# A seven-product scheme for the down projection of a convolutional FFN, in fp32 on one NeuronCore

## What is computed

```python
D_FF = 2816
def conv_ffn(a, w_up, conv_w, w_down):
    g, u = jnp.split(dwconv3(a @ w_up, conv_w), 2, axis=-1)
    return (jax.nn.silu(g) * u) @ w_down

# in both layers of second_block:
h = h + g2 * conv_ffn(modulate(rms_norm(h, norm_ffn[i]), sh2, sc2), ffn_w_up[i], ffn_conv[i], ffn_w_down[i])
```

## Time and profile before

| | kernel before |
|---|---|
| median of 3 runs | 2008.44 us |
| the profiled execution: time / span | 2007.74 / 2006.0 us |
| PE busy | 1888.5 us (94%), 19216 matmul records |
| PEld busy | 1634.6 us (81%), 19216 load records |
| DVE busy | 823.5 us (41%), 1430 instructions |
| ACT busy | 371.6 us (19%) |
| mean granted TensorE clock | 0.976 of 2.4 GHz |
| HBM read | 463.29 MB, 231 GB/s over the span |

### The profile page before, as it was taken

One profiled execution on the slowest core, in us unless ns is written; L12 is line 12 of the kernel. 1 busy time (PEld: TensorE's weight loads), 2 busy tenths in 40 slices (PEclk: granted clock), 3 DMA queues, 4 the chain that ended last, 5 costly groups with the idle time before them and its releaser, 6 DMA issues.

```text
span 2006.0 us, 41961 instructions
## 1 busy us (share of the span) xinstructions
PE 1888.5 (94%) x19216; PEld 1634.6 (81%) x19216; DVE 823.5 (41%) x1430; ACT 371.6 (19%) x691; POOL 25.1 (1%) x24
## 2 busy tenths in 40 slices
PE   6999987989998999997999999999999999999999
PEld 3788776889997788686899996667888778878878
DVE  3868786100004767764000004665675111233210
ACT  3012232100003021322000013361111110021100
POOL 0000200000000000200000000000000000000000
PEclk8999988999999999998999999999999999999999
DMA  9994546699994581562999991204787444434320
GB/s 356 387 385 147 203 166 266 251 375 405 420 411 172 206 316 63 210 237 103 376 387 422 422 392 54 84 2 163 260 295 278 139 145 139 155 126 160 124 74 21
DMA packets 180598, 466.09 MB, mean 232 GB/s; under 512 B 5152, under 2 KB 55680, under 8 KB 172288
## 3 DMA queue, kind: packets, MB, share of 16 engines
q1 hardware_dynamic: 180192, 463.83, 62.1%
q10 hardware_dynamic: 288, 0.52, 0.1%
HBM read 463.29 MB, written 1.05 MB: 231 GB/s over the span
## 4 chain that ended last, share of the span: by engine, by line
PE 86%; DVE 9%; ACT 2%; issue 2%; DMA 1%; SPq 1%; DVEq 0%; ACTq 0%
PE pair L366 84%; DVE AR L1517 2%; DMA ring<-in_ada_w 1%; PE pair L1005 1%; DVE RST L1572 1%; DVE AR L1755 1%; ACT AR L1239 1%; DVE XH L1517 1%; SPq L257 0%; DVE AR L1765 0%; PE pair L874 0%; DVE AR L1769 0%; DVE XH L1756 0%; DVE AR L1809 0%; DVE XH L1579 0%
## 5 line engine op out<-in xcount | busy, mean ns | idle before, releaser
L366 PE MATMUL pair<-AR,ring 128*64 128x88 f32 (+1 forms) x13632 | 772.0, 254 | 30.1 <-issue 16.2
L366 PEld LDWEIGHTS pair<-AR,ring 128*64 128x64 f32 (+1 forms) x13632 | 727.7, 143 | 72.9 <-issue 23.2
L366 PE MATMUL pair<-XH,ring 128*128 128x256 f32 (+1 forms) x3328 | 752.2, 387 | 19.1 <-ACT XH L1140 17.3
L366 PEld LDWEIGHTS pair<-XH,ring 128*128 128x128 f32 (+1 forms) x3328 | 629.9, 191 | 126.2 <-issue 30.1
L2004 DVE TENSOR_TENSOR AR<-AR,pair 128x352 f32<-128x352 f32 x32 | 16.7, 521 | 427.8 <-PE pair L366 427.8
L1517 DVE SCALAR_TENSOR_TENSOR AR<-ring,CACT,AR 128x512 f32<-128x512 f32 x245 | 184.2, 752 | 8.7
L366 PE MATMUL pair<-AR 128*64 128x128 f32 (+5 forms) x768 | 103.0, 330 | 6.5 <-ACT AR L1406 3.3
L366 PEld LDWEIGHTS pair<-AR 128*64 128x64 f32 (+3 forms) x768 | 76.8, 165 | 18.5 <-issue 4.2
L2105 DVE SCALAR_TENSOR_TENSOR AR<-pair,VEC,AR 128x255 f32<-128x255 f32 x88 | 41.9, 476 | 114.4 <-ACT AR L1431 114.4
L1339 ACT ACTIVATE AR<-pair 128x704 f32 (+1 forms) x32 | 24.4, 762 | 308.7 <-PE pair L366 308.7
L1431 ACT ACTIVATE AR<-pair,VEC 128x256 f32<-128x256 f32 x88 | 36.5, 465 | 224.0 <-PE pair L366 224.0
(11 more groups left out here) (256 smaller groups left out, 1091.1 us busy)
## 6 DMA issues: line engine op xcount, KB each, us to landing
ring<-in_ada_w SPq DMA_DIRECT2D x48, 2048.0 KB, 13.0
ring<-in_w_gate SPq DMA_DIRECT2D x32, 2048.0 KB, 10.7
ring<-in_w_up SPq DMA_DIRECT2D x32, 2048.0 KB, 10.8
ring<-in_w_down SPq DMA_DIRECT2D x32, 2048.0 KB, 11.3
ring<-in_ffn_w_up SPq DMA_DIRECT2D x44, 1024.0 KB, 7.6
ring<-in_w_in SPq DMA_DIRECT2D x18, 2048.0 KB, 14.2
ring<-in_ffn_w_down SPq DMA_DIRECT2D x8, 2048.0 KB, 7.8
ring<-in_sc_w_in SPq DMA_DIRECT2D x6, 2048.0 KB, 7.9
```

The costliest lines, as they stand in the source:

```text
L366: return pe.matmul(o, lhsT, rhs, start=start, stop=stop, **kw)
```

## The change

`A` and each chunk of weights are seen as 2 x 2 blocks. For the activations, the index k is the parity of the input tile and h the half of the tokens (128 each); for a weight chunk, k is the same parity and m one half (256 columns) of the 512 output features. For each output half and each of the three chunks (now 4, 4 and 3 pairs of input tiles) seven products of quarter size are formed, in place of the eight of the plain scheme: with sums of weight blocks (S1 = a21 + a22, S2 = S1 - a11, S3 = a11 - a21, S4 = a12 - S2) and sums of activation blocks (T1 = b12 - b11, T2 = b22 - T1, T3 = b22 - b12, T4 = b21 - T2). VectorE makes the weight sums for every chunk (`weight_sums`, 4 operations of up to 128 x 1024) and the activation sums once for each of three groups of an FFN (`token_sums`, 4 operations of up to 128 x 512). Each matmul has a 64-column weight tile and 128 moving columns. The seven products accumulate over the chunks in separate regions of PSUM; `output` adds each of them into `X`, 20 VectorE operations for each half. Half 0 now writes banks 4 to 7, half 1 banks 1 to 5.

The waits are new as well: half 0 starts when the convolution has read tiles up to 19 instead of 21; products 6 and 3 wait for sums of weights; product 4 of half 1's first chunk waits for half 0's output; the DVE starts half 1's output after product 5 of the last chunk. VectorE's program has `token_sums` ahead of the convolution of tiles 10 and 18, and the first chunk's weight sums ahead of tile 20. Besides, some semaphores without use are dropped and two of the start are joined.

The diff, cut to this:

```diff
+TH = S // 2
+DOWN_PAIRS = ((0, 4), (4, 4), (8, 3))
+
+
+BANK_OF = [{1: (4, 4), 6: (4, 4), 7: (5, 5), 5: (5, 5), 2: (6, 6), 3: (6, 6), 4: (7, 7)},
+           {1: (1, 1), 6: (1, 1), 7: (2, 2), 5: (2, 2), 2: (3, 3), 3: (3, 3), 4: (4, 5)}]
+SECOND_IN_BANK = (6, 5, 3)
...
+        SX = [AR[:, 1024 * b:1024 * b + 1024].rearrange("p (t n) -> p t n", t=4) for b in (6, 7, 8)]
+        T1 = XH[:, 2048:2048 + 11 * TH].rearrange("p (t n) -> p t n", t=11)
+        T2 = AR[:, 9 * 1024:9 * 1024 + 11 * TH].rearrange("p (t n) -> p t n", t=11)
+        T4 = AR[:, 9 * 1024 + 11 * TH:9 * 1024 + 22 * TH].rearrange("p (t n) -> p t n", t=11)
+
+        def token_blocks(a, n):
+
+            v = a[:, 0:2 * n * S].rearrange("p (t k h n) -> p t k h n", k=2, h=2, n=TH)
+            return [v[:, :, k, h, :] for k in range(2) for h in range(2)]
+
+        def weight_blocks(c, n):
+
+            v = ring[c % RING][:, 0:2 * n * 512].rearrange("p (t k m n) -> p t k m n", k=2, m=2, n=S)
+            return [v[:, :, k, m, :] for m in range(2) for k in range(2)]
+
+        def of_product(hf, n, m):
+
+            b = BANK_OF[hf][n][m]
+            a = 512 * (b % 2) + S * (n in SECOND_IN_BANK) + TH * m
+            return pair[b // 2][:, a:a + TH]
+
...
-                A = AR[:, 0:22 * N].rearrange("p (t n) -> p t n", n=N)
+                b11, b12, b21, b22 = token_blocks(AR, 11)
                 for hf in range(2):
 
-                    if hf == 0:
-                        pe.wait_ge(s["cv_conv"], 2 * (done_tiles + 22))
-                    for k, (a, nk) in enumerate(((0, 8), (8, 8), (16, 6))):
+                    pe.wait_ge(s["cv_conv"], 2 * (done_tiles + (20, 22)[hf]))
+                    for k, (p0, n_p) in enumerate(DOWN_PAIRS):
                         c = ck(f"down{3 * hf + k}", l)
+                        i = 6 * l + 3 * hf + k
+                        a11, a12, a21, a22 = weight_blocks(c, n_p)
+                        tail = hf == 1 and k == 2
+
+                        def product(n, left, right):
+
+                            for m in range(2):
+                                o = of_product(hf, n, m)
+                                opens = k == 0 and n not in SECOND_IN_BANK and BANK_OF[hf][n].index(BANK_OF[hf][n][m]) == m
+                                for t in range(n_p):
+                                    for j in range(0, P, CT):
+                                        last = mm(o[j:j + CT, :], left[:, t, P * m + j:P * m + j + CT],
+                                                  right[:, p0 + t, :], opens and t == 0, False, skip_group_check=True)
+                                if tail and (n, m) in ((2, 1), (3, 1), (4, 0)):
+                                    last.then_inc(s["out_tile"], 1)
+                            return last
+
                         arrived(c)
-                        w = view(c, nk, 512)
-                        pe.wait_ge(s["ff_act"], done_tiles + a + nk)
-                        for m in range(4):
-                            for t in range(nk):
-                                last = mm(banks(4 * hf)[m][:, 0:N], w[:, t, m * P:m * P + P], A[:, a + t, :],
-                                          a + t == 0, a + t == 21)
-                            if hf == 1 and k == 2 and m < 3:
-                                last.then_inc(s["out_tile"], 1)
-                        done(last)
+                        pe.wait_ge(s["ff_act"], done_tiles + 2 * (p0 + n_p))
+                        product(1, a11, b11)
+                        pe.wait_ge(s["tokens_summed"], 3 * l + k + 1)
+                        pe.wait_ge(s["weights_summed"], 4 * i + 3)
+                        product(6, SX[1], T2)
+                        product(7, a21, b12)
+                        product(5, SX[0], T1).then_inc(s["sum_used"], 1)
+                        product(2, a12, b21)
+                        pe.wait_ge(s["weights_summed"], 4 * i + 4)
+                        product(3, SX[2], b22)
+                        if hf and k == 0:
+                            pe.wait_ge(s["x_done"], 8 * (6 + 2 * l) + 4)
+                        done(product(4, a22, T4))
...
 
+            def token_sums(l, g):
+
+                p0, n = DOWN_PAIRS[g]
+                V.wait_ge(s["ff_act"], 22 * l + 2 * (p0 + n))
+                b11, b12, b21, b22 = [b[:, p0:p0 + n, :] for b in token_blocks(AR, 11)]
+                t1, t2, t4 = [t[:, p0:p0 + n, :] for t in (T1, T2, T4)]
+                link(V.tensor_tensor(t1, b12, b11, ALU.subtract))
+                step(V.tensor_tensor(b12, b22, b12, ALU.subtract))
+                link(V.tensor_tensor(t2, b22, t1, ALU.subtract))
+                V.tensor_tensor(t4, b21, t2, ALU.subtract).then_inc(s["tokens_summed"], 1)
+
+            def weight_sums(l, n, since=0, upto=4):
+
+                i, c = 6 * l + n, ck(f"down{n}", l)
+                n_p = DOWN_PAIRS[n % 3][1]
+                a11, a12, a21, a22 = weight_blocks(c, n_p)
+                s1, s2, s4 = [x[:, 0:n_p, :] for x in SX]
+                if since == 0:
+                    V.wait_ge(full[c % RING], 16 * (c // RING + 1 + extra(c)))
+                    if i:
+                        V.wait_ge(s["sum_used"], i)
+                    V.tensor_tensor(s1, a21, a22, ALU.add).then_inc(s["weights_summed"], 1)
+                    V.wait_ge(s["weights_summed"], 4 * i + 1)
+                    V.tensor_tensor(s2, s1, a11, ALU.subtract).then_inc(s["weights_summed"], 1)
+                    V.tensor_tensor(a21, a11, a21, ALU.subtract).then_inc(s["weights_summed"], 1)
+                if upto == 4:
+                    V.wait_ge(s["weights_summed"], 4 * i + 2)
+                    if n:
+                        multiplied(c - 1)
+                    V.tensor_tensor(s4, a12, s2, ALU.subtract).then_inc(s["weights_summed"], 1)
+
+            def fold(Q, t, last):
+
+                V.wait_ge(s["squares_ready"], 8 * 7 + t + 1)
+                ins = V.tensor_tensor(Q[:, 0, :], Q[:, 0, :], Q[:, t, :], ALU.add)
+                if last:
+                    ins.then_inc(s["folded"], 1)
+                else:
+                    link(ins)
+
+            def output(X, l, hf, Q=None):
+
+                c = ck(f"down{3 * hf + 2}", l)
+                changed = [steps[0]] * 4
+
+                def add(n, f, halves):
+
+                    t = 4 * hf + f
+                    V.wait_ge(s["dve_step"], changed[f])
+                    q = of_product(hf, n, f % 2)
+                    x = X[:, t, :]
+                    if halves == 2:
+                        q = q.rearrange("p (a n) -> p a n", a=1).to_broadcast([P, 2, TH])
+                        x = x.rearrange("p (a n) -> p a n", a=2)
+                    else:
+                        x = x[:, TH * halves:TH * halves + TH]
+                    return V.scalar_tensor_tensor(x, q, MOD[:, 1, l, 40 + t, 0:1], x, ALU.mult, ALU.add)
+
+                def part(n, f, halves):
+                    step(add(n, f, halves))
+                    changed[f] = steps[0]
+
+                if hf:
+                    V.wait_ge(s["sum_used"], 6 * l + 6)
+                else:
+                    multiplied(c)
+                for f in range(4):
+                    part(1, f, 2)
+                for f in range(4):
+                    part(6, f, 1 if f < 2 else 2)
+                for f in (2, 3):
+                    part(7, f, 2)
+                for f in range(4):
+                    part(5, f, 1)
+
+                if hf:
+                    V.wait_ge(s["out_tile"], 3 * (3 + 2 * l) + 2)
+                for f in range(2):
+                    part(2, f, 0)
+                for f in range(2):
+                    add(3, f, 1).then_inc(s["x_done"], 1)
+                if Q is not None:
+                    fold(Q, 4, False)
+                if hf:
+                    V.wait_ge(s["out_tile"], 3 * (3 + 2 * l) + 3)
+                add(4, 2, 0).then_inc(s["x_done"], 1)
+                if Q is not None:
+                    fold(Q, 5, False)
+                multiplied(c)
+                add(4, 3, 0).then_inc(s["x_done"], 1)
+                if Q is not None:
+                    fold(Q, 6, True)
+
             def ffn(l, n, X, H, N):
                 norm(n, X, H, 1, l, 1)
                 A = AR[:, 0:22 * N].rearrange("p (t n) -> p t n", n=N)
@@ -2095,6 +2228,10 @@
                 for j in range(22):
                     if j % 2 == 0 and j < 20:
                         modulation(BEFORE[f"up{j // 2 + 1}", l], bank(4 * ((j // 2 + 1) % 2) + 3))
+                    if j in (10, 18):
+                        token_sums(l, j // 8 - 1)
+                    if j == 20:
+                        weight_sums(l, 0)
                     b0 = (4 * ((j // 2) % 2) + 2 * (j % 2))
                     tmp = CVT[j % 2]
                     for h in range(2):
@@ -2112,10 +2249,18 @@
                 if l == 0:
                     coef(1, 1, 0, (1, 1, 11))
                     coef(1, 1, 1, (1, 1, 11))
+                token_sums(l, 2)
```

(30 more changed lines are left out.)

8 lines of the change are left out of this document (1 added, 7 removed).

## The result

The changed kernel takes 1983.78 us (median of 4 runs, 1983.47 to 1986.11) against 2009.83 for the kernel before, now with four runs: a ratio of 0.9875, 95% interval 0.9858 to 0.9893. The forecast was 1984 in 1978 to 2000, and a gain of 24.4 us; the medians give 26.1. The profiled execution of the changed kernel has a span of 1984.3 us.

What follows compares the result with a forecast made beforehand. The prediction took TensorE's matmul stream, with what stands before and behind it, as the bound: 9.7 (starts) + 22.8 (streams) - 4.1 - 3.4 (ends) - 0.6 (tile shapes) = 24.4 us saved, giving 1984 us, range 1978 to 2000.

Steps and rivals of the forecast that it cites:

- the start: At both down projections TensorE's wait of 4.86 us goes, 9.7 us in all; without it 5.2 us of fallen clock go too.
- the cover: Spare time of VectorE's sums before the up chunk's end: 1.2 us in the first FFN, 0.7 in the second.
- The stream: Down projection matmuls: 1232 records of 54.5 ns, 67.1 us an FFN; both streams save 22.8 us, 5.2 of it clock.
- the burst: Window attention's 16 records of the same shape, giving at most 64.4 ns a record, change of tile shape included.
- The change of tile shape: Switching weight tile shapes on TensorE costs at most 0.16 us each, four times, 0.6 us.
- The middle: Within the down stream, sums and half 0's output (6.6 us) come in time: no stop, or 0.6 us per FFN without overlap.
- The ends: Behind each FFN's stream, VectorE's last additions and the output transfers come later, costing 4.1 and 3.4 us.
- the norm's fallen clock: Behind the first FFN, the longer wait may add 0 to 1.5 us at a fallen clock; taken as 0.
- Instruction supply: Rival, chance 0.12: in the written-out down stream, instruction packets stop TensorE, costing 12 us: 1996.
- VectorE late: Rival, chance 0.13: VectorE's operations last half as long again, near 5 us lost per FFN: 1995, with 1990 to 2000.
- Narrow tiles that eat the eighth: Rival, chance 0.05: down stream records take 61.7 ns, the stream is 151.9 us again, 6.8 us gain remains: 2002.
- exposed loads: Rival, chance 0.07: 64-column weight loads don't hide behind 128 moving columns in the down stream: 2049 half exposed, 2115 fully.

Runs made afterwards that it cites:

- e1: The kernel before with only the halves' PSUM banks exchanged and half 0 waiting for convolution tiles up to 19, eight products kept: 1994.98 us.
- e2: The changed kernel with half 0 waiting again for the convolution of tiles 20 and 21, seven products kept: 1994.09 us.
- e3: The changed kernel with weight tiles of 128 columns instead of 64: 1987.95 us.
- e5: The changed kernel, but in half 1's last chunk VectorE starts adding products 1 and 6 after product 6 instead of product 5: 1975.72 us.
- e10: The kernel of e5 run once more, beside a rerun of the changed kernel on the same chip: 1980.11 us.
- e6: The kernel of e5 with the output leaving in two transfers of four tiles each instead of five and three: 1975.51 us.
- e4: The changed kernel with weight tiles of 32 columns instead of 64: 2005.50 us.
- e8: The changed kernel with three of the four weight sums of each chunk formed twice: 1990.82 us.

## Why the prediction was right

**What bounds the kernel, and the start.** TensorE's stream and what stands before and behind it set the time, as the prediction had it. Both waits went, no other took their place, and the clock stayed at 1.00. e1 and e2 show the start's worth from both sides: 15.7 and 14.2 us of the stretch, for 9.7 + 5.2 = 14.9 forecast (by the medians 12.7 and about 10). On VectorE the cover was to be 1.2 us in the first FFN and 0.7 in the second, measured from the fourth sum's end. It was 1.6 in the first and 3.6 in the second (the fourth sum at 1905.41 + 1.22 against 1910.25), where the token sums ran in time that VectorE had free before the last up chunk; I had laid all 7.8 us into one idle stretch.

**The stream.** The 54.5 ns a record, read off a line between 88 and 256 moving columns, was 54.4; the upper bound of the burst, 64.4, held a change of shape. The two streams last 67.5 us each to the end of the last record (1627.41 - 1559.94 and 1977.71 - 1910.25), so 22.1 us are saved, where I had 22.8: my 67.1 left out the last record's latency. The change of tile shape, put at up to 0.16 us each, is 0.1 at the stream's start (e3).

**The weight loads.** The Trainium skill (page TensorE: Matmul & The Clock Gate, part "Packing small matmuls") has weight loads overlap running matmuls only where the row groups differ, and by that the change would have been slower. This trace disagrees: in 1560 to 1575 us matmuls and loads are each busy 15.00 of 15.00, and a product of 32 loads and 32 matmuls takes 1.74 us, while its 32 load records span 1.78 us of the same time.

**The middle.** The fourth sum of chunk 3 was to end 0.7 us before product 3; it ended 1.1 before it. Chunk 4's were to leave 0.8 and left 1.4.

**The ends.** The last addition was to come 71.2 and 69.9 us after the stream's start, and came at 71.1 and 69.9. The second FFN was to end at 74.1 with both transfers on the way together, and ended at 74.05; the 384 KB took 3.7 us to land for 2.5 before. e5 shows the cause: VectorE's additions, begun earlier, took 2.1 us off each end. Mis-sized in the sum is the norm behind the first FFN: both matmuls by ones (four records) now stand together behind the fold, at a granted clock of 0.50, and take 2.08 us. From the last addition to the next stage's first matmul it is 6.0 us instead of 4.7: 1.3 more, where I had 0.6. In e3 the same four records take 1.18 us at a better clock, so the order of the matmuls costs about what I had, and 0.9 us of the 2.08 is the clock.

**What I left at nothing** and wasn't: the norm's fallen clock. I had it between 0 and 1.5 us of loss. From 1637.08 to 1910.25 the changed kernel takes 273.2 us for the same work as 275.3 before (1643.22 to 1918.50), 2.1 less. The clock over 9.4 us behind this norm was 0.82 instead of 0.69. It can't be put down to the change: the first stage behind the norm takes 86.1 us before and 84.8 in both executions of the changed kernel, but 85.7 and 84.5 in two executions of one kernel, e5 and e10, and 86.2 in e6. The price of the fallen clock behind the same norm differs by over 1 us between executions.

The sum, measured in the profiled executions: 9.7 (starts) + 22.1 (streams) - 4.4 and 3.1 (ends) + 2.1 (clock behind the norms) = 26.4 of 26.5 us, for 24.4 forecast. Without the 2.1 it is 24.3, so the forecast's mechanism and its sizes hold. That the median of 1983.78 meets the 1984 so closely is luck in part: the medians of one kernel differ by 1 to 5 us (1982.71 and 1983.78 for the changed kernel, 1975.72 and 1980.11 for that of e5), and the 2.1 us of clock weren't in the forecast.

**The rivals.** Instruction supply: not in this kernel, but e4 met it at twice the demand, and nearly all of it beside weight traffic. So to compare 7.0 with 5.8 us was right, and the 12 us weren't due. The Trainium skill's statement (page Runtime: NRT & Kernel Launch, section "Instruction fetch mechanics"), that crossing an instruction block is mostly hidden, agrees with the changed kernel, and not with e4's 13.6 us. VectorE late: e8 shows what it would have taken, 3.7 us more for each full chunk, to lose 8.9. Narrow tiles that eat the eighth, and exposed loads: the stream's rate excludes both; e3 adds that even the full width costs only 3 ns.

## What to carry to other kernels

Split a large edit into what it saves in work and what it frees in order: here two waits of 4.86 us, with the clock that falls behind them, made half of the gain or more and needed only that the next stage write other banks and wait for less. When a scheme trades matmuls for sums, list each sum's earliest start and latest end beside the matmul stream; the sums are free where the list has room, and what remains is the addition of the results behind the last matmul, which should start with the first product that is complete. The rate of a shape that the trace doesn't hold can be estimated from a line between two shapes that it does hold; here the line between two long streams gave the 54.4 ns a record that were measured, and the short burst only an upper bound of 64.4.

## What the runs showed of the hardware

- In fp32 with 128 moving columns, 128 weight columns take 109 ns as two tiles of 64, 112 as one of 128, and no less as four of 32. A whole fp32 matmul is two such records, so it takes twice that. Loads and matmuls are busy at the same time (15.00 of 15.00 us).
- Instruction packets of 16 KB reached TensorE at least each 3.6 us without other traffic (1.6 us of stops in 62), and each 4.4 us on average beside 2 MB weight transfers (DMA share 0.41; 13.6 us of stops in 80, single ones up to 3.1). A stream that asks for one in 7.0 us had no stop.
- A wait of 4.86 us on TensorE costs 2.0 to 3.2 us more in granted clock behind it (0.65 and 0.53 over some 5.5 us in e2, 0.83 and 0.50 in the earlier trace rows). Behind the same norm that price differs by 1.2 us between two executions of one kernel (e5, e10).
- Twenty of VectorE's additions from PSUM, eight of 256 columns with a broadcast source and twelve of 128, take 6.33 us beside a full matmul stream, for 6.6 worked out from plain ones: the broadcast source costs nothing that shows.
- A change between 128- and 64-column weight tiles costs 0.1 us at the start of the stream (13.99 against 13.90 us).
